# Token factors of four norms multiplied in behind the matrix products, in a two-block transformer layer

## The reference, cut to what matters

```python
def rms_norm(x, g):
    y = x * lax.rsqrt(jnp.mean(x * x, axis=-1, keepdims=True) + EPS)
    return y * g
...
# first block
x = x + mixed @ w_out
h = rms_norm(x, ffn_norm)
x = x + (silu(h @ w_ffn_gate) * (h @ w_ffn_up)) @ w_ffn_down
x = rms_norm(x, final_norm)
# second block
x = x + 0.5 * swiglu(rms_norm_2(x, ffn1_norm), ffn1_w_gate, ffn1_w_up, ffn1_w_down)
h = rms_norm_2(x, mix_norm)
...                                 # attention branches, gates, merged
x = x + merged @ w_out
x = x + 0.5 * swiglu(rms_norm_2(x, ffn2_norm), ffn2_w_gate, ffn2_w_up, ffn2_w_down)
x = x + sigmoid(rms_norm_2(x, ple_norm) @ w_ple_gate) * (p @ w_ple_proj)
```

## Time and profile before

| what | value |
|---|---|
| three runs | 1224.12, 1231.58 and 1223.18 us; median 1224.12 us |
| profiled execution, its own time | 1222.96 us |
| its span, first to last instruction | 1220.8 us |
| TensorE busy | 1136.5 us, 93% of the span |
| VectorE, ScalarE, GpSimd busy | 770.2, 711.8 and 57.0 us |
| mean granted clock of TensorE | 0.964 of full speed |
| memory traffic | 187.10 MB, mean 153 GB/s |

### The profile page before, as it was taken

One profiled execution on the slowest core, in us unless ns is written; L12 is line 12 of the kernel. 1 busy time (PEld: TensorE's weight loads), 2 busy tenths in 40 slices (PEclk: granted clock), 3 DMA queues, 4 the chain that ended last, 5 costly groups with the idle time before them and its releaser, 6 DMA issues.

```text
span 1220.8 us, 19865 instructions
## 1 busy us (share of the span) xinstructions
PE 1136.5 (93%) x7388; PEld 1024.5 (84%) x7388; DVE 770.2 (63%) x1160; ACT 711.8 (58%) x1148; POOL 57.0 (5%) x58
## 2 busy tenths in 40 slices
PE   4999998999989999979999998999899989999987
PEld 3898897889978888968888896987768978888977
DVE  4788787536776665557767555445537776766564
ACT  4447655485567774447766443556757467775453
POOL 0000000001400000100000010000000300000110
PEclk9999999999989999999999997998889989999989
DMA  5344433224535454544544563432213535554542
GB/s 204 123 147 156 140 132 114 104 104 173 186 126 206 174 199 150 189 150 148 196 177 180 166 201 111 165 139 90 83 69 139 176 135 195 183 188 157 200 152 104
DMA packets 31995, 187.10 MB, mean 153 GB/s; under 512 B 4032, under 2 KB 7488, under 8 KB 14144
## 3 DMA queue, kind: packets, MB, share of 16 engines
q1 hardware_dynamic: 31936, 186.28, 43.4%
HBM read 184.43 MB, written 1.05 MB: 152 GB/s over the span
## 4 chain that ended last, share of the span: by engine, by line
PE 78%; DVE 10%; ACT 6%; issue 3%; DMA 1%; POOL 1%; SPq 0%; ACTq 0%; DVEq 0%; POOLq 0%
PE acc L581 70%; PE area_a L581 4%; PE area_t L581 3%; DVE wlo L1379 2%; ACT L1042 1%; ACT whi L1042 1%; DVE xr L1499 1%; ACT he L1042 1%; DMA raw<-in_w_dn 1%; POOL mixed L1907 1%; DMA raw<-in_w_projT_a 1%; PE area_t L813 1%; DVE s_after L1873 0%; DVE st L1518 0%; ACT gates L1042 0%
## 5 line engine op out<-in xcount | busy, mean ns | idle before, releaser
L581 PE MATMUL acc<-hs,whi 128*128 128x256 f32 (+1 forms) x2784 | 693.4, 332 | 34.7 <-DVE hs L1494 20.9
L581 PEld LDWEIGHTS acc<-hs,whi 128*128 128x128 f32 x2784 | 471.1, 195 | 80.0 <-issue 29.3
L581 PE MATMUL acc<-hs,wlo 128*128 128x256 f32 x1920 | 528.1, 286 | 0.0
L1042 ACT ACTIVATE whi<-raw 128x1024 fp32r<-128x1024 f32 (+2 forms) x378 | 350.0, 976 | 83.1 <-PE acc L581 73.4
L1379 DVE TENSOR_TENSOR wlo<-raw,whi 128x1024 fp32r<-128x1024 f32 (+3 forms) x258 | 269.5, 1086 | 177.7 <-ACT whi L1042 177.3
L581 PEld LDWEIGHTS acc<-hs,wlo 128*128 128x128 f32 x1920 | 371.7, 194 | 10.9
L581 PE MATMUL acc<-hid,whi 128*128 128x512 f32 (+1 forms) x660 | 185.7, 350 | 0.3 <-DVE wlo L1379 0.2
L581 PE MATMUL acc<-hid,wlo 128*128 128x256 f32 x528 | 145.5, 281 | 0.0
L1452 DVE TENSOR_TENSOR wlo<-raw,whi 128x1024 fp32r<-128x1024 f32 x120 | 141.7, 1222 | 3.8
L581 PEld LDWEIGHTS acc<-hid,whi 128*128 128x128 f32 x660 | 113.9, 188 | 17.7 <-DVE wlo L1379 0.9
L1042 ACT ACTIVATE tmp<-acc 128x256 f32<-128x256 f32 x150 | 57.4, 382 | 98.3 <-PE acc L581 98.3
(11 more groups left out here) (294 smaller groups left out, 1038.0 us busy)
## 6 DMA issues: line engine op xcount, KB each, us to landing
raw<-in_w_gu SPq DMA_DIRECT2D x66, 1024.0 KB, 4.8
raw<-in_w_dn SPq DMA_DIRECT2D x48, 704.0 KB, 4.1
raw<-in_w_up SPq DMA_DIRECT2D x10, 1024.0 KB, 4.8
raw<-in_w_gates1b SPq DMA_DIRECT2D x8, 1024.0 KB, 4.8
raw<-in_w_out SPq DMA_DIRECT2D x8, 1024.0 KB, 4.8
raw<-in_w_qk SPq DMA_DIRECT2D x8, 1024.0 KB, 4.8
raw<-in_w_gates SPq DMA_DIRECT2D x8, 1024.0 KB, 4.8
raw<-in_w_projT_b SPq DMA_DIRECT2D x7, 1024.0 KB, 4.9
```

The lines of the kernel that those rows point to most:

```text
L581: return nc.tensor.matmul(out, w, m, start=start, stop=stop, skip_group_check=True)
L1042: return nc.scalar.activation(out, in_, f, **kw)
```

## The change

`norm3` is no longer a step of its own. For `norm1`, `norm2`, `norm5` and `norm6` (`LATE_NORMS`) `x` times the channel gain alone is split into `hs`, chunk by chunk, while the blocks in front of the norm are still being added to `x`: `residual_used` on ScalarE, `late_low` on VectorE. `first_tile` takes these unnormed chunks. The product with ones (`square_sums`) stands behind the first tile, and root and reciprocal (`mean_root`, `mean_factor`) in the second body of `gate_up`. The token factor `xr` is then multiplied in later: onto the gate sum before `Silu` (`scale_gate`, once for each tile), onto the result of the down-projection (line 1477, or 1474 for a block summed in one region), and onto the blocks of `w_pg`. `norm2` and `norm3` together become one factor: a second ring of squares, of x times the final gain, gives a second mean, and the first factor `xr1` is multiplied into `x` in the down-projection behind it. The split of `mixed` gets buffers of its own (`ms1`, `ms2`), since `hs` is now written during `w_out`.

```diff
     tiles(4)
     phase("w_gu0", KF); phase("w_dn0", 16)
-    steps("norm2", "norm3")
+    steps("norm2")
...
 NORMS = [s for k, s in ORDER if s in [f"norm{i}" for i in range(7)]]
+LATE_NORMS = ("norm1", "norm2", "norm5", "norm6")
...
+            def square_sums(name):
+
+                t = take_t(name)
+                i = SUMMED_NORMS.index(name)
+                pe.wait_ge(S("squares_added"), (KD - 2) * (i + 1))
+                mm(t[:, 0, :], ones, sq_sum[:], True, False)
+                pe.wait_ge(S("square"), KD * (i + 1))
+                m = mm(t[:, 0, :], ones, sq_ring[:, (KD - 1) % 2, :], False, True)
+                if name == "norm2":
+                    pe.wait_ge(S("squares2_added"), KD - 2)
+                    mm(t[:, 1, :], ones, sq_sum2[:], True, False)
+                    pe.wait_ge(S("square2"), KD)
+                    m = mm(t[:, 1, :], ones, sq_ring2[:, (KD - 1) % 2, :], False, True)
+                m.then_inc(S("t_full"), 1)
 
...
+                if (g in HS_BEFORE or g in MS_BEFORE) and name != "w_fvl":
                     first_tile(g, first_of[name][0])
+                    if name == "w_pg":
+                        square_sums("norm6")
...
             def gate_up(f):
                 g0, n0 = FIRST[f"w_gu{f}"], BLOCKS[f"gu{f}"]
                 first_tile(g0, n0)
+                square_sums(("norm1", "norm2", "norm5")[f])
...
+                if SUMMED_NORMS[i] == "norm2":
+                    if k >= 2:
+                        act.wait_ge(S("squares2_added"), max(k - 2, 1))
+                    g = VEC["final_norm"] + k
+                    fn(sq_ring2[:, k % 2, :], x[:, k, :], ACT.Square, scale=vec[:, g:g + 1])\
+                        .then_inc(S("square2"), 1)
+
+            def residual_used(n):
+
+                if n in LATE_BLOCK:
+                    name, k = LATE_BLOCK[n]
+                    act.wait_ge(S("block_freed"), n + 1)
+                    fn(hs[:, k, 0:T], x[:, k, :], ACT.Copy, scale=late_gain(name, k)).then_inc(S("hs_hi"), 1)
+                square(n)
+
+            def mean_root(name):
+
+                act.wait_ge(S("t_full"), TURN_T[name] + 1)
+                if name == "norm2":
+                    fn(xr1[:], area_t[:, 0, :], ACT.Sqrt, scale=1.0 / D, bias=epsb[:, 0:1])\
+                        .then_inc(S("first_root"), 1)
+                    act.wait_ge(S("means_joined"), 1)
+                    fn(xr[:], xr[:], ACT.Sqrt, scale=1.0 / D).then_inc(S("t_freed"), 1)
+                else:
+                    fn(xr[:], area_t[:, 0, :], ACT.Sqrt, scale=1.0 / D, bias=epsb[:, 0:1]).then_inc(S("t_freed"), 1)
 
             def tile(g):
                 split_high(g + 1, 0)
                 split_high(g + 1, 1)
+                if g == FIRST["w_pg"]:
...
+                def body(t, j, first=False, second=False, last=False):
 
                     if not first:
-                        act.wait_ge(S("block_freed"), t * 2 + (n0 - 1))
+                        if second:
+                            copy_half(0, 0, 1)
+                            mean_root(("norm1", "norm2", "norm5")[f])
+                            split_next(t, j, 0)
+                            split_next(t, j, 1)
+                        act.wait_ge(S("gate_scaled"), t + KF * f)
                         fn(sbuf[:, 1 - j, :], gbuf[:, 1 - j, :], ACT.Silu).then_inc(S("silu"), 1)
-                        copy_half(t - 1, 1 - j, 1)
-                    if not last:
+                        if not second:
+                            copy_half(t - 1, 1 - j, 1)
...
+                if 0 <= n - BLOCKS["dn1"] < KD:
+                    k = n - BLOCKS["dn1"]
+                    g = VEC["final_norm"] + k
+                    link(v.scalar_tensor_tensor(x[:, k, :], x[:, k, :], vec[:, g:g + 1], xr1[:], ALU.mult, ALU.mult))
                 if n not in ONE and (n in SUM_DEST or n in RESIDUAL):
...
+                    if n in LATE_BLOCK and LATE_BLOCK[n][0] in ("norm1", "norm5"):
+                        v.scalar_tensor_tensor(x[:, k, :], bank[:, 0:T], scale, x[:, k, :], ALU.mult, ALU.add)\
+                            .then_inc(S("block_freed"), 1)
                     else:
-                        link(v.tensor_tensor(t, t, x[:, k, :], ALU.add))
-                    v.scalar_tensor_tensor(x[:, k, :], bank, scale, t, ALU.mult, ALU.add)\
-                        .then_inc(S("block_freed"), 1)
+                        if t is None:
+                            t = tmp[:, n % 4, :]
+                            link(v.tensor_tensor(t, bank[:, 0:T], xr[:], ALU.mult))
+                        else:
+                            link(v.tensor_tensor(t, t, bank, ALU.add))
+                            link(v.tensor_tensor(t, t, xr[:], ALU.mult))
+                        v.scalar_tensor_tensor(x[:, k, :], t, scale, x[:, k, :], ALU.mult, ALU.add)\
+                            .then_inc(S("block_freed"), 1)
+                    if n in LATE_BLOCK and k:
+                        late_low(n - 1)
                 elif n in GATED:
                     u = GATED[n]
...
+                elif n in SUM_DEST and n < BLOCKS["pgp"] + 8:
+                    v.tensor_tensor(SUM_DEST[n], bank[:, 0:T], xr[:], ALU.mult).then_inc(S("block_freed"), 1)
                 elif n in SUM_DEST:
...
+                def scale_gate(t, j):
+
+                    dve.wait_ge(S("block_freed"), t * 2 + (n0 + 1))
+                    v.tensor_tensor(gbuf[:, j, :], gbuf[:, j, :], xr[:], ALU.mult).then_inc(S("gate_scaled"), 1)
...
                     if not first:
                         sum_halves(t - 1, 1 - j, 1)
+                        if second:
+                            mean_factor(("norm1", "norm2", "norm5")[f])
+                            scale_gate(0, 0)
+                            split_next(t, j, 0)
+                            split_next(t, j, 1)
...
+                        if not first:
+                            scale_gate(t, j)
...
+                if f == 1:
+                    link(v.reciprocal(xr1[:], xr1[:]))
...
+            def late_low(n):
+                name, k = LATE_BLOCK[n]
+                dve.wait_ge(S("hs_hi"), KD * HS_ORDER.index(name) + k + 1)
+                v.scalar_tensor_tensor(hs[:, k, T:2 * T], x[:, k, :], late_gain(name, k),
+                                       hs[:, k, 0:T].bitcast(F32), ALU.mult, ALU.subtract).then_inc(S("hs_lo"), 1)
...
+            def mean_factor(name):
+                if name == "norm2":
+                    dve.wait_ge(S("t_full"), TURN_T[name] + 1)
+                    dve.wait_ge(S("first_root"), 1)
+                    link(v.tensor_tensor(xr[:], xr1[:], xr1[:], ALU.mult))
+                    v.scalar_tensor_tensor(xr[:], xr[:], EPS * D, area_t[:, 1, :], ALU.mult, ALU.add)\
+                        .then_inc(S("means_joined"), 1)
                 dve.wait_ge(S("t_freed"), TURN_T[name] + 1)
...
+                if name in LATE_NORMS:
+                    late_low(RESIDUAL_OF[name][1] + KD - 1)
+                    return
...
```

More of the change, by code:

```diff
@@ L1384, in read_block @@
             def read_block(n):
-                if n in ONE and n in SUM_DEST and n not in GATED and n < BLOCKS["pgp"] + 8:
+                if n in ONE and n in SUM_DEST and n not in GATED and n < BLOCKS["pgp"]:
                     halves[0] += 1
@@ L1438, in tile @@
                 split_low(g + 1, 1)
+                if g == FIRST["w_pg"]:
+                    mean_factor("norm6")
                 for n in ENDING.get(g, []):
@@ L1468, in body @@
                             .then_inc(S("hid_value"), 1)
-                    if not last:
+                    if not last and not second:
                         split_next(t, j, 0)
@@ L1487, in down @@
             def down(f):
+                if f == 1:
+                    link(v.reciprocal(xr1[:], xr1[:]))
                 for g in range(FIRST[f"w_dn{f}"], FIRST[f"w_dn{f}"] + 16):
                     tile(g)
+            HS_ORDER = ("norm0", "norm1", "norm2", "norm4", "norm5", "norm6")
             def hs_low(name, k, src):
-                base_ = KD * HS_STARTS.index(name.replace("half", "split"))
-                dve.wait_ge(S("hs_hi"), base_ + k + 1)
+                dve.wait_ge(S("hs_hi"), KD * HS_ORDER.index(name) + k + 1)
@@ L1515, in row_max @@
+                for k in (KD - 2, KD - 1):
+                    hs_low(name, k, tmp[:, k % 4, :])
             def row_max(tag, sc, tt):
```

146 lines of the change are left out of this document (79 added, 67 removed).

## The result

Side by side on one chip the changed kernel takes 1184.38 us (median of 4 runs, 1184.03 to 1185.07), the kernel before 1225.28 (4 runs, 1223.18 to 1231.58). The ratio is 0.9646, with a 95% interval from 0.9619 to 0.9672. The forecast was 1189, a gain of 34.85. The medians side by side are 40.9 us apart. So the direction and the mechanism at the four places held, and the gain was forecast too small by some 6 to 8 us. Two more comparisons, on other chips, gave 0.9638 and 0.9657.

The account below looks back on a forecast made before the run. TensorE bounds the kernel, busy 1136.5 of 1220.8 us, so only its stops and slow stretches give time. Gains 36.95 - 0.2 - 0.45 - 1.45 = 34.85 from 1224.12 give 1189; 8-in-10 range 1184 to 1199.

Parts of the forecast that it names:

- the four places: Stops at `norm1`, `norm2` with `norm3`, `norm5`, `norm6`: removing each stop and the slow tile behind it gives together 35.75 us.
- the product with ones: Stays on TensorE at the changed norms: 0.59 us for one of the pair, 1.2 for two, 2.4 for four at `norm2`.
- The stops and the slow clock: At the four changed norms TensorE should not stop and run at full clock: gains of 7.4, 13.8, 7.35 and 7.2 us.
- The end: Behind the `w_pg` blocks: the table load before the sigmoid is done during waiting, a VectorE product replaces a copy; 1.2 us gained.
- The entry of the second down-projection: The reciprocal of `xr1` comes ahead of the first low parts and delays TensorE: 1.45 us charged, bounds 0 and 1.75.
- The following 0.3 as a stop: Sign at the second down-projection's start: a TensorE stop of about 1.2 us, then another of 0.3.
- The last block at `norm4`: The norm stays in front, so the last block's scaling stands on the path: +0.45 us.
- The openings: First tiles of each feed-forward: tight but no stop, except at `norm2`, 0.5 against 0.4 of slack; 0.2 us charged in all.
- The table load: Load between square and root in the second bodies: taken as 1.28 us from the trace, without the skill's drain of about 1.38.
- the first rival: Feed-forward starts: later `Silu` delays the fourth tile's weights, stops of 1.3 us three times, more at `norm2`; 1194 us, chance 0.12.
- The loop as the bound: Gate-and-up loops: VectorE and ScalarE's turn outgrows TensorE's 5.6 us; gain gone at 6.1, 1248 us at 6.5; chance 0.04.

Follow-up runs that it names:

- at 5.87: The changed kernel with two more VectorE products, into a buffer nobody reads, in each of the 66 gate-and-up tiles: 1215.57 us.
- at 6.20: The changed kernel with three more VectorE products, into a buffer nobody reads, in each of the 66 gate-and-up tiles: 1241.59 us.
- the moved reciprocal: The changed kernel with the reciprocal of `xr1` moved from ahead of the second down-projection's first low part to just ahead of the first block using it: 1190.11 us.

## What the prediction had right, and the steps that failed

- **The steps that failed.** Two terms of the sum, not the mechanism at the four places. The larger one: **the scatter of the kernel before, and with it the half clock in the parts that the change does not touch, was put at nothing**. The forecast subtracts its sum from 1224.12, a median of three runs, and its range has no term for it. The 34 runs of before that stand beside the later experiments have a median of 1228.0 and go from 1222.75 to 1232.78. They follow the mean granted clock: the three runs at 0.964 have a mean span of 1221.2 us, the three at 0.956 one of 1229.3. What the touched places gave in the traces, 38.2 us (below), would have made 1224.12 - 38.2 = 1185.9, inside the range; the other 5.1 of the 43.3 us no stretch shows as a gain of the change, and they lie within this scatter. The smaller one: **the product with ones** was charged at 1.2 and 2.4 us and measured 0.86 and 1.74. Which of the untouched stops makes most of the scatter was read behind `norm4` only and stays open for the rest.
- **The stops and the slow clock.** Right in all four places, in mechanism and nearly in size: 8.35, 14.1, 8.55 and 9.05 us for 7.4, 13.6, 7.35 and 8.4. What was mis-sized is the term for the product with ones. I took 0.59 us from the first stop as the time of one and made it 1.2 and 2.4. There it stood alone between two waits; where they stand in a dense row, two take 0.86 and four 1.74. That is 3 x 0.34 + 0.66 = 1.7 us of the missing gain. The other 1.6 us at these places (0.35 of them at the end), and 0.4 in the last down-projection, are small shares that I can read but did not test; in the first pair of traces 0.1 and 0.5 us of them lie in the two `w_out` parts.
- **The end**: 1.2 forecast, 1.55 read (29.8 to 28.25 us behind the first `w_pg` tile); no table load ahead of the sigmoid. Right.
- **The entry of the second down-projection**: 1.45 charged, 1.41 measured by taking it away, with the stop of 1.14 where it was expected. The following 0.3 as a stop did not show. I had read it off the row at 685.98 in the earlier trace rows as a wait for a load; that row names a wait of 0.17 us for a low part of the weights, so the part with the load is not shown.
- **The last block at `norm4`**: 0.45 charged, too little. From the last product of the down-projection to the first behind the norm it takes 7.83 us, 6.79 before: 1.04. I counted the scaling by `xr` (0.42) and left out that `x` times `xr1` stands ahead of it on VectorE. That one started only at 717.88, behind a low part of weights, and took 0.95 us instead of 0.48, beside an addition of GpSimd. The step of the prediction that was wrong here is the path: two instructions stand on it, not one. VectorE, then GpSimd:

```profile
716.72 1.24 DVE L1444 TENSOR_TENSOR wlo<-raw,whi 128x1040 fp32r<-128x1040 f32 x1
717.88 0.95 DVE L1458 SCALAR_TENSOR_TENSOR x<-x,vec,xr 128x256 f32<-128x256 f32 x1
718.86 0.42 DVE L1474 TENSOR_TENSOR tmp<-acc,xr 128x256 f32<-128x256 f32 x1
719.32 0.43 DVE L1478 SCALAR_TENSOR_TENSOR x<-tmp,x 128x256 f32<-128x256 f32 x1
```

```profile
716.87 1.67 POOL L2032 TENSOR_TENSOR sq_sum<-sq_sum,sq_ring 128x256 f32<-128x256 f32 x1 [7.03 <-ACT sq_ring L1072]
```

- **The openings**: 0.2 charged, 0.24 measured, one stop in the second feed-forward and none in the two others. The rival with stops of 1.3 us there did not come true.
- **The table load.** The opening above shows the load at 349.14 for 1.28 us and the root at 350.44, again without a gap, and so does the second one (352.82, `Silu` at 354.12). The Trainium skill ("ScalarE: Activation LUTs", What ACT_TABLE_LOAD costs) gives each such switch a drain of about 1.38 us beside the load; the trace does not agree, since no more than 0.05 us is left on either side. By the estimate in the first rival, made with such a drain, each opening would have stopped for 1.3 us, and the only stop is the 0.24 above. The rows had been the right choice.
- **The rest of the gain is not shown to be the change's.** The touched places give 39.25 - 1.04 = 38.2 us. The runs gave 40.9, 45.2 and 40.0 on three chips. The 2 to 7 us between are within what the kernel before and the changed kernel each scatter by: their runs span 10.0 and 8.7 us, and the stretches behind `norm4` alone vary by 8 us between traces of one program. In the traces of the two kernels the untouched stretches overlap, so no gain of theirs can be read. The forecast needed a term for this of 0 with a width of some 5 us, and the range (5 us below the forecast) had no room for it.
- **The loop as the bound**: did not come. Its point of decision was given as a turn of 6.1 us. The runs put it a little lower: at 5.87 the gain is down to 1% (ratio 0.9905), at 6.20 the kernel is 1.1% slower, and a straight line between them crosses at about 6.0, for the exit costs 4.2 to 5.4 us a feed-forward that I had not counted.

## What to carry to other kernels

Where TensorE stops for a chain of small instructions (sum, root, reciprocal, scale), let it go on with unscaled data and put the factor in behind a product whose result is read anyway. Price the stop, the slow clock behind it, and what that slow clock hides, and then ask whether the helpers' spare time in the following loop pays back their debt before the loop ends. Where the stop can't be removed, products that nobody reads can keep the clock up, in these traces without making the stop longer; and judge small edits by the stretch they touch, not by the median, as long as another stop lets the clock scatter by more than they are worth.

## What was not expected of the hardware

- The same products, issued without a pause behind the same stop of 5.13 us, ran at half clock for 7, 11 and 15 us in three executions of one program, and for 23 with the moved reciprocal. In these three executions the `w_fvl` products took 20.0, 21.8 and 23.5 us, at full clock 16.65.
- With eleven products in that stop the granted clock stayed at 1.00 behind it. The Trainium skill ("TensorE: Matmul & The Clock Gate", Part 1: The HAM clock gate) says that it is activity that releases the clock; the trace agrees.
- In the second down-projection VectorE scales `x` eight times. The first two took 0.48 us, with GpSimd idle (at 661.86 and 670.45); the other six took 0.95 or 0.96, each beside an addition of GpSimd, such as the one at 677.49. A product that reads a bank of TensorE's results (`up<-acc,gates`) took 0.42 with GpSimd at work and without.
- On ScalarE an instruction with a pointer as its scale took 0.51 us (`hs<-x,vec`, 0.49 where it overlaps the instruction ahead), and 0.42 with a constant, at 128x256 elements.
- In the kernel before, ScalarE loaded a table ahead of every second `Silu` of the loops, 30 times in all; in the changed kernel it does so once in each loop. That is 27 loads, 34.6 of the 39 us by which ScalarE's busy time fell. As far as the rows show, it gave no time back: at the turns without a load ScalarE waited about as long, 1.25 us, for `gbuf`, and the turn was TensorE's. Why the loads stood there is not shown. In before:

```profile
370.74 0.42 ACT L1042 ACTIVATE sbuf<-gbuf 128x256 f32<-128x256 f32 x1 [1.25 <-DVE gbuf L1458]
...
375.10 1.28 ACT L1042 ACT_TABLE_LOAD   x1
376.40 0.42 ACT L1042 ACTIVATE sbuf<-gbuf 128x256 f32<-128x256 f32 x1
```
